# A due-time table for a streaming encoder: where the second prompt tile's merges stand among the gathers

## The reference

```python
h = rmsnorm(x, g_norm[l, 0]) * (1 + sc1) + sh1
z = h @ w_in[l]                       # 18 chunks of 128 columns
# pooling mixer, gated MLP over 128-chunks, differential attention, each on its share of z
x = x + gt1 * (concat([ya, yb, o]) @ w_out[l])
h2 = rmsnorm(x, g_norm[l, 1]) * (1 + sc2) + sh2
x = x + gt2 * peer_ffn(h2, w_pq[l], sub_keys[l], u_tab[l], v_tab[l])
```

```python
s = einsum(q, sub_keys)               # two lists of 128 scores
sv, si = top_k(s, 16)
cand = sv[0][:, None] + sv[1][None]   # 256 sums
tv, ti = top_k(cand, 16); eidx = the expert numbers; gate = softmax(tv)
a = einsum('tkd,td->tk', u_tab[eidx], hx)
out = einsum('tk,tkd->td', gate * gelu(a), v_tab[eidx])
```

## Time and profile before

| | us |
|---|---|
| median of 3 runs | 2542.1 |
| the runs | 2540.8, 2542.1, 2552.6 |
| the profiled execution | 2547.1 |
| its span, first to last instruction | 2545.3 |
| PE busy | 1338.0 (53%) |
| DVE (VectorE) busy | 1395.2 (55%) |
| ACT (ScalarE) busy | 295.8 (12%) |
| POOL (GpSimd) busy | 1458.7 (57%) |
| mean DMA rate | 381 GB/s |

### The profile page before, as it was taken

How to read it: one execution, slowest core, us unless ns; L and a number is a source line. 1 busy time by engine, 2 the same in 40 slices (tenths; PEclk the granted TensorE clock), 3 DMA queues, 4 the chain that set the end, 5 groups by cost and what they waited for, 6 DMA issues and landing times.

```text
span 2545.3 us, 22274 instructions
## 1 busy us (share of the span) xinstructions
PE 1338.0 (53%) x7726; PEld 749.4 (29%) x7726; DVE 1395.2 (55%) x3292; ACT 295.8 (12%) x637; POOL 1458.7 (57%) x1541
## 2 busy tenths in 40 slices
PE   3788594678534035446565458489530023333555
PEld 2656383554114022123221137366110000000111
DVE  1114879856658974446441268855849964444000
ACT  1222242311001011000000023221000000000000
POOL 0000255546776655756667675445777767777774
PEclk7879796789757555776777669599655555555766
DMA  8698799999999999999999999899999999999998
GB/s 305 236 373 288 312 350 381 341 365 409 403 408 408 409 404 375 401 395 409 410 383 409 410 409 409 305 380 362 369 410 410 410 408 409 409 405 409 402 409 331
DMA packets 265894, 969.16 MB, mean 381 GB/s; under 512 B 38036, under 2 KB 40084, under 8 KB 262456
## 3 DMA queue, kind: packets, MB, share of 16 engines
q0 software_dynamic: 221184, 805.40, 80.4%
q1 hardware_dynamic: 42256, 161.25, 16.5%
q10 hardware_dynamic: 2344, 1.09, 0.2%
HBM read 962.36 MB, written 5.27 MB: 380 GB/s over the span
## 4 chain that ended last, share of the span: by engine, by line
DMA 33%; PE 26%; POOL 16%; DVE 15%; issue 7%; ACT 2%; ACTq 1%; SPq 1%; POOLq 0%; DVEq 0%
DMA ring<-in_u,eU 15%; DMA ring<-in_v,eV 13%; POOL ring L393 11%; DVE ring L712 10%; PE ps L1150 7%; PE ps L1353 6%; POOL ring L388 5%; PE ps L1190 4%; PE ps L1328 2%; PE ps L1047 1%; DMA wring<-in_wpq 1%; DMA wada<-in_wada 1%; ACTq L418 1%; PE ps L1167 1%; PE ps L1194 1%
## 5 line engine op out<-in xcount | busy, mean ns | idle before, releaser
L712 DVE CUSTOM_DVE_ANT_0 ring<-ring,ps 128x1024 f32<-128x1024 f32 x768 | 914.0, 1219 | 498.5 <-DMA ring<-in_u,eU 371.7
L388 POOL DMA_INDIRECT ring<-in_u,eU x768 | 723.8, 942 | 725.2 <-DVE eU L1013 252.7
L393 POOL DMA_INDIRECT ring<-in_v,eV x768 | 734.2, 956 | 337.7 <-issue 168.6
L1150 PE MATMUL ps<-ring,Wd 128*32 128x512 f32 x3072 | 575.3, 887 | 652.3 <-DMA ring<-in_v,eV 645.2
L1150 PEld LDWEIGHTS ps<-ring,Wd 128*32 128x32 f32 x3072 | 116.5, 139 | 1041.6 <-issue 1037.8
L1353 PE MATMUL ps<-h,wring 128*128 128x128 f32 (+1 forms) x1024 | 201.0, 356 | 26.2 <-DMA wring<-in_wpq 22.3
L1353 PEld LDWEIGHTS ps<-h,wring 128*128 128x128 f32 x1024 | 171.9, 213 | 80.2 <-issue 44.1
L1190 PE MATMUL ps<-h,wring 128*128 128x128 f32 (+1 forms) x768 | 139.9, 345 | 76.5 <-ACT zv L400 48.0
L1190 PEld LDWEIGHTS ps<-h,wring 128*128 128x128 f32 x768 | 125.2, 206 | 90.1 <-ACT zv L400 48.2
L909 DVE MAX8 sv<-sc 128x8 f32<-128x128 f32 x192 | 50.0, 288 | 164.9 <-ACT sc L400 162.0
L730 DVE SCALAR_TENSOR_TENSOR x<-ps,mods,x 128x128 f32<-128x128 f32 x32 | 8.6, 344 | 190.8 <-PE ps L1158 190.8
(11 more groups left out here) (166 smaller groups left out, 1089.6 us busy)
## 6 DMA issues: line engine op xcount, KB each, us to landing
wada<-in_wada SPq DMA_DIRECT2D x24, 2048.0 KB, 10.2
wring<-in_win SPq DMA_DIRECT2D x72, 512.0 KB, 7.7
wring<-in_wpq SPq DMA_DIRECT2D x64, 576.0 KB, 8.3
wring<-in_wout SPq DMA_DIRECT2D x32, 512.0 KB, 7.5
ring<-in_u,eU POOLq DMA_INDIRECT x768, 9.8
ring<-in_v,eV POOLq DMA_INDIRECT x768, 8.4
wring<-in_ckT SPq DMA_DIRECT2D x8, 512.0 KB, 9.2
wring<-in_cv SPq DMA_DIRECT2D x8, 512.0 KB, 7.1
```

The source lines that it names most:

```text
L388: g.indirect_dma_start(ring[p % NR][:], None, a["u"], bass.IndirectOffsetOnAxis(ap=eU[t % 3][:, i:i + 1], axis=0)).then_inc(ld_r[p % NR], 16)
L393: g.indirect_dma_start(ring[p % NR][:], None, a["v"], bass.IndirectOffsetOnAxis(ap=eV[t % 3][:, tok:tok + 1], axis=0)).then_inc(ld_r[p % N ...
L712: nc.vector.tensor_tensor_reduce(ring[p % NR][:], ring[p % NR][:], ps[:, 0:2, :].rearrange("p b d -> p (b d)"), 1.0, 0.0, ALU.mult, ALU.ad ...
L1150: ins = mm(ps[QUAD * q:QUAD * q + QUAD, 2 + half, :], Wd[:, QUAD * q + c, :], ring[at4[q] % NR][:, half * 512:(half + 1) * 512], start=(c ...
```

## The change

`tick_at` treats the second prompt tile's merge apart. All other steps of a front, the first prompt tile's merge included, are spread over the unit's span as before, but with the second merge left out of the sum of costs, so each of them falls somewhat later. The second merge's eight steps are spread over the positions from 16 behind the end of the span to 8 ahead of that tile's own first u block. Front 2 begins behind that, at position 385 instead of 283, and ends where it ended.

```diff
-SPAN = ((0, 0), (0, AT["u", T0[1] * P]), (RES_OF[0] + 1, AT["v", 2 * P] + HEAD - 16), (RES_OF[2] + 1, AT["u", T0[3] * P]))
+SPAN = ((0, 0), (0, AT["u", T0[1] * P]), (AT["u", 2 * P] + 1, AT["v", 2 * P] + HEAD - 16), (RES_OF[2] + 1, AT["u", T0[3] * P]))
 
 
 def tick_at(n, k):
     a, b = SPAN[n]
-    cost = COST[:T_EXP + 8 * NT[n]]
-    return a + (b - a) * sum(cost[:k + 1]) // sum(cost)
+    last = T_EXP + 8
+    if k >= last:
+        t = T0[n] + 1
+        return b + 16 + (AT["u", t * P] - b - 24) * (k + 1 - last) // 8
+    return a + (b - a) * sum(COST[:k + 1]) // sum(COST[:last])
```

## The result

The changed kernel is slower by 0.28%: 2552.4 us median of 20 runs against 2544.3 of the kernel before in as many, ratio 1.0028, 95% interval 1.0020 to 1.0036. That is 7 us (5 to 9). The forecast was 3 us faster, with "no change one can tell" the likeliest class; the class holds, the sign does not. Two disturbed executions of the whole study, one of 2640.3 us of the kernel before and one of 2556.0 of e7_again, both at a lower granted clock, are left out.

A forecast was written before the change was run, and what follows sets the result against it. The kernel was taken as its bytes at the DMA ceiling plus time lost below it. Terms -10 -15 +8 +11 +3 = -3 us gave 2544 us for the profiled execution, 2539 against the median; range 2512 to 2570.

The forecast's parts named there:

- no change one can tell: Whole kernel: a time neither faster than 2529.4 nor slower than 2554.8 us, chance 0.46.
- Part 3: Front 2, in 343 positions instead of 445: some POOL and PE waits join, a loss of 3 us (0 to 8).
- Part 1, layer 0: First prompt front in layer 0: 28 more blocks pass beside it, a gain of 10 us.
- Part 1, layer 1: Prompt front 3 in layer 1: 25 more blocks pass beside it, eU then comes last, a gain of 15 us.
- Part 2: Second tile's merge among solo u blocks, where DVE has little spare time: a loss of 8 us in layer 0, 11 in layer 1.
- the dots in the way: Layer 1's prompt front: with the dots and the weights in the way, the gain would be 5 us.
- The 6.0: Gather behind POOL's wait for eU in layer 1: 6.0 us to land behind an empty queue.
- Layer 0's 8 us: Late second merge in layer 0: block 384 lands at 891.7 instead of 883.7, a loss of 8 us.
- Rival B: Solo u stretches pay the second merge in full, 17 us per layer: 23 us slower, 2565 us, chance 0.17.
- The 16 us: Threshold for Rival B: it decides once the two merges cost over 16 us more than the fronts gain.
- C: Prompt fronts late by as much as the added batches and dots, no block gained: 22 us slower, 2564 us, chance 0.11.
- A: Prompt fronts' gain at its limits, all lost DMA time outside attention goes: 26 us faster, 2516 us, chance 0.26.

The follow-up runs named there:

- e7_again: On top of e1, front 3 keeps its old positions up to its output norm and only then goes slower; 0.9912 of the kernel before, 2521.3 us.
- e3: Changed kernel with the other steps of the prompt fronts back at their positions of before, second merge still late; 1.0086 of the kernel before, 2562.0 us.
- e6: On top of e1, front 3 (layer 1) keeps the old pace, front 1 the new one; 0.9975 of the kernel before.
- e1: Changed kernel with the second merge's eight steps moved to where u and v blocks alternate; 0.9955 of the kernel before, 2530.3 us.
- e4: Kernel before with only front 2 beginning at 385 instead of 283; 0.9999 of the kernel before.

## Why the prediction was wrong

**The frame held for Parts 1 and 2.** Their gains and losses showed as DMA time below 409.6 GB/s in the stretches where they were forecast. Part 3's did not: its stretch shows 6 us of gain that no timed run has. The parts, forecast and measured:

| step | forecast | measured | from |
|---|---|---|---|
| Part 1, layer 0 | -10 | -10 | after against e3, less layer 1 |
| Part 1, layer 1 | -15 | -5 | e6 against e1 |
| Part 2, both merges | +19 | +22 | e3 against e4 |
| Part 3, front 2 | +3 | 0 | e4 against before |
| sum | -3 | +7 | |

**The step that failed is Part 1, layer 1.** The mechanism was the right one: eU of tile 4 becomes what block 1001 waits for (6.59 us, at 1831.03), and the gain is the 28 us by which eU was early, less the front's slip. The term that was mis-sized is that slip. I put it at 12 us, that is 6.25 batches of 1.9 us on PE, and it is 23.4, which leaves 28 - 23.4 = 5. The trace of after has

```profile
1506.64 0.77 PE L1193 MATMUL ps<-h,wring 128*128 128x256 f32 x1 [5.75 <-ACT h L491]
...
1651.09 1.22 PE L1331 MATMUL ps<-h,wring 128*128 128x256 f32 x2 [3.14 <-ACT rs L407]
...
1706.44 0.89 PE L1356 MATMUL ps<-h,wring 128*128 128x256 f32 x3 [4.03 <-ACT h L491]
...
1803.56 0.40 DVE L961 CAST sif<-si 128x256 bf16<-128x256 uint32 x1
```

for z, output projection, query projection and merge, where before has, with 1782.93 of the earlier trace rows behind them,

```profile
1509.41 1.19 PE L1190 MATMUL ps<-h,wring 128*128 128x256 f32 x2 [5.75 <-ACT h L488]
...
1641.62 0.79 PE L1328 MATMUL ps<-h,wring 128*128 128x256 f32 x1 [3.97 <-ACT rs L404]
...
1689.91 2.30 PE L1353 MATMUL ps<-h,wring 128*128 128x256 f32 x5 [3.90 <-ACT h L488]
```

From z to the output projection 144.5 us instead of 132.2, to the query projection 55.4 instead of 48.3, to the merge 97.1 instead of 93.0: the front takes 23.4 us longer, not 12. The last two are the batches, as forecast: four more ahead of the query projection (+7.1; 4 x 1.9 = 7.6) and 2.25 more ahead of the merge (+4.1; 2.25 x 1.9 = 4.3), together 11.2 of the 12. The first, +12.2, I had left out: the dots that the slower pace puts ahead of the steps of z and attention. By the positions it is 12 more between the first z step and the output projection (85 instead of 73), and 12 x 1.14 = 14 us. I had counted 6, and weighed them in DMA terms only, as 7 us of work that carries 8 us of gathers, and so as neutral. For the front they are not, since each stands ahead of a step that the chain waits for. The text named "the dots in the way" as the case of a 5 us gain; that case is what happened. e7_again shows it: with those dots behind the attention the way from z to the output projection is back at 132.1 us, the front is 10 us shorter and the kernel 12 us faster. The profile was to show the projections above 395 GB/s; 1706 to 1798 has 385 in the changed kernel.

In layer 0 the same slip is there (end of scores 618.0 before, 637.1 after), 19 us instead of the 13 forecast, and it didn't matter: eU had 38 us of room, and is there at 663.6, 7 us ahead of the first issue that needs it (670.5). That issue is 12 us earlier than before.

**Part 2** was right in place and kind. POOL's waits for eU were put at 10 to 15 us and are 13.1 and 13.4, and eU comes 131.5 us (tile 2) and 132.1 us (tile 5) behind the first dot after the residual, worked out as 129.4 and 132.1. The lost time went up by 13.2 and 11.0, forecast 8 and 11. One of the two gathers behind the wait at 2037.7 took 4.4 us to land, the other 5.3, not 6.0. The 6.0 was no case of an empty queue: it was read in 1780 to 1810, in a slice with 369 GB/s. Layer 0's 8 us was the weaker figure: it rested on taking 18.7 us of weight traffic off an in-flight queue of 17 us. Rival B, 17 us for each, did not come. The 16 us from which it was to decide had a wrong sign in it: 12.7 us slower, less Part 3's 3 or 4, is 9.

By the Trainium skill (SBUF — State Buffer, section "SBUF: two separate sides") a DVE operation in a two-port mode, or one with two SBUF inputs, locks GpSimd out; the merge's two operations of L1008, which read `taf` or `tbf` and `iob` from SBUF, are of the second kind. The trace of after agrees: beside the first, a gather issue took 2.48 us instead of 0.94.

```profile
848.63 2.29 DVE L1008 TENSOR_TENSOR eq<-taf,iob 128x2048 bf16<-128x2048 bf16 x1
...
849.25 2.48 POOL L391 DMA_INDIRECT ring<-in_u,eU  x1 [0.30 <-issue]
...
856.04 0.93 POOL L391 DMA_INDIRECT ring<-in_u,eU  x1 [3.04 <-DVE adot L715]
```

But soon behind it POOL waits 3.04 us for a dot, and beside the second, at 872.81, it is waiting for eU anyway, so nothing here shows a price for it.

**Part 3**: 0 us instead of 3. Positions 400 to 640, 900 to 1270 us, lose 8 us in the changed kernel, not the 10 to 20 forecast.

**The rivals.** C, the fronts late by as much as they win, is the nearest to what happened in layer 1, where 23 us of slip left 5 of 28, and wrong for layer 0 and the whole. A came nowhere near. Of the 10 us between forecast and measurement, layer 1's Part 1 is 10, Part 2 is 3 and Part 3 is 3 the other way; that the last two cancel is luck.

**A version that beats both** came out of it: second merge among the pairs, front 3 unslowed up to its output norm (e7_again), 0.9912 (0.9903 to 0.9920), 22 us under the kernel before and some 30 under the changed one.

## What to carry to other kernels

When a schedule by hand is stretched, count the work that moves ahead of each step of the latency chain, not only whether that work pays for itself in bandwidth: 12 us of dots in front of z and attention cut this change's gain in layer 1 from some 15 us to 5. Before moving work to a stretch, take the spare time per unit there (here 0.14 us of DVE per u block against 1.4 per pair of u and v) and what comes last for the next unit: the same 27 us of merge cost 22 us for two in the solo stretch and some 6 among the pairs, by the lost time there. And when one step in a direction helps, the next need not: 25% fewer positions for the part of each prompt front up to its output norm cost 33 us.

## What had not been expected of the hardware

A gather issued behind 13.4 us without an issue landed in 4.4 us (block 1152 of the changed kernel), the shortest of the cases that I had looked at; the next one took 5.3; behind some nine others it was 12.0. The row of the two:

```profile
DMA to landing us min/median/max: 4.4/4.9/5.3
```

Otherwise the ceiling of 409 to 410 GB/s was the same in the traces of all runs, on the three chips of the experiments.
